# Two 16-head attentions of a float32 model: outputs ahead of the next copy on VectorE, and their transposes tile by tile

## The chip, the core and the metric

The kernel runs as one launch on one core of a Trainium2 chip. The metric is the device time of that launch in microseconds (us), as the median over runs. PE is TensorE, DVE is VectorE, ACT is ScalarE, POOL is GpSimd, SP is the queue that issues the DMAs.

## What is computed

A residual stream of 256 tokens by 1024 channels goes through four layers in float32: two with attention and a gated feed-forward network, and two with a mixer and a mixture of 32 experts. The part that the change touches is the attention of the first two layers (16 attention maps each), cut to what matters:

```python
# layer 0: 8 dilated heads and 8 forgetting heads of 64 channels
p = softmax(q @ k.T + mask)                   # mask differs by head
o[:, a*64:(a+1)*64] = p @ v[:, a]             # 16 heads -> 1024 channels
h = h + o @ w_out
# layer 1: 8 differential heads, each of two maps, v of 128 channels
o = (softmax(q1 @ k1.T + mask) - lam * softmax(q2 @ k2.T + mask)) @ v
o = rms_norm(o, subln_g) * (1 - lam_init)     # per head, over its 128 channels
h = h + o.reshape(256, 1024) @ w_out
```

The mixers of layers 2 and 3 hold, among other things, an attention of 8 latent heads each.

## The kernel before

Each engine has a program written out by hand, and semaphores join them; an engine takes its instructions in that order. Weights come as chunks of 1 MB through a ring of three buffers. For a product to be exact enough, each operand is split into a high and a low part (ACT writes the high one, DVE subtracts for the low one), and PE does three products for one (`product`).

**The attention** (`attention` in the programs of DVE and PE, `softmaxes` in that of ACT). For a map a, PE multiplies the scores (`pair_scores`, two maps at a time), DVE adds the mask and takes the row maximum (`scores`, L873), ACT takes the exponential and the row sum (L533), PE transposes the probabilities in three pieces (`turn`, L1495), DVE copies them out of PSUM (`probs`, L883) after a reciprocal of the row sums (L880), and PE multiplies them by v (`values`, L1505 to L1507). After every second map DVE scales the pair's two outputs out of PSUM into `tok` (`outputs`: L901 for heads of 64 channels; L906 and L908, with lambda, for the differential heads). The loop of DVE over the maps is

```python
for a in range(n):
    if a + 2 < n:
        scores(a + 2)
    if a + 1 < n:
        probs(a + 1)
    outputs(a)          # does something for odd a only
```

and that of PE, for each a: the scores of a later pair (at even a), `turn(a + 1)`, `values(a)`. In the differential attention ACT squares a finished pair's outputs after the exponential of an odd map (`head_squares`, L546: the pair before the one whose exponential it has just done), and POOL turns the sums into a factor and multiplies it in (L437, L438, L442); for the last pair DVE does the last part (`last_head_norm`, L935). The differential attention also multiplies its reciprocals of odd maps by lambda on DVE (L888).

**After the attention** the 256 x 1024 outputs in `tok` have to be transposed for the projection: 8 tiles of 128 channels, 2 transposes each (`transposes`, L1421). PE waits there until all of `tok` is ready. A tile k goes to the bank and half that `t_place(k)` gives; four tiles share two banks' worth of events. ACT reads each tile from PSUM as its high part (`high`, L508), DVE as its low part (`low`, L834); PE's projection (`out_projection`, `group`, L1358 to L1360) waits for the low part of tile k before its product k. The first half of the output channels uses banks 0 and 1 and two chunks of weights, the second half banks 2 and 3 and two more. ACT and DVE split those later chunks (`plain` and DVE's `out_projection`) after their tiles.

All four attentions, those of the latent heads too, use the same `attention` functions; only the two with 16 maps use `pair_scores`.

Of the kernel before, what the change touches and what calls it, by code (L numbers as in the profile page):

```python
# [18 lines left out]
F32 = mybir.dt.float32  # L19
F32R = mybir.dt.float32r  # L20
ALU = mybir.AluOpType
ACT = mybir.ActivationFunctionType
# [123 lines left out]
T_BASE = [sum(T_TILES[:q]) for q in range(len(T_TILES) + 1)]  # L146
T_BANKS = [2 * (n // 3) for n in T_TILES]
T_BANK_BASE = [sum(T_BANKS[:q]) for q in range(len(T_BANKS) + 1)]
# [3 lines left out]
def t_place(k):  # L152
    return 2 * (k // 4) + k % 2, k % 4 // 2

T_L0, T_L0O, T_F0, T_L1, T_L1O, T_F1 = range(6)
# [6 lines left out]
def build(nc, x, stream, router, small, const, fgain, out):  # L162
    es = ExitStack()
    with es:
# [302 lines left out]
        def _(act):  # L467
# [31 lines left out]

            def high(q, dst, gain, free):  # L500

                act.wait_ge(chunk_used, free) if free else None
                for k in range(T_TILES[q]):
                    b, at = t_place(k)
                    act.wait_ge(t_done, T_BANK_BASE[q] + b + 1)
                    if at:
                        act.wait_ge(t_low, T_BASE[q] + k - 1)
                    nc.scalar.activation(dst[:, k, :], B[4 + b][:, at * S:at * S + S], ACT.Copy, scale=gain(k)).then_inc(t_high, 1)  # L508

# [195 lines left out]
            projections(C_DIFF, 4, 16)  # L705
            softmaxes(16, range(2, 16), head_squares)
            head_squares(17)
            high(T_L1O, xh, lambda k: gain_sub[:, 0:1], C_DIFF_OUT)
            plain(C_DIFF_OUT, 3)
# [87 lines left out]
        def _(dve):  # L797
# [31 lines left out]

            def low(q, dst, hi, gain):  # L830
                for k in range(T_TILES[q]):
                    b, at = t_place(k)
                    dve.wait_ge(t_high, T_BASE[q] + k + 1)
                    stt(dst[:, k, :], B[4 + b][:, at * S:at * S + S], gain(k), hi[:, k, :].bitcast(F32),  # L834
                        ALU.mult, ALU.subtract).then_inc(t_low, 1)
# [29 lines left out]
            def attention(first, n, masks, scale, dv, diff, between=None, score_bank=0, turned_bank=6, score_banks=2):  # L865
# [11 lines left out]
                def probs(a):  # L877
                    dve.wait_ge(p_tr, first + a + 1)
                    step[0] += 1
                    nc.vector.reciprocal(rden[:, a, :], den[:, a, :]).then_inc(dve_step, 1)  # L880
                    if a >= 2:
                        dve.wait_ge(pv_done, first + a - 1)
                    nc.vector.tensor_copy(prT[:, a % 2, :], B[turned_bank + a % 2][:, 0:384]).then_inc(pT_ready, 1)  # L883

                    if diff and a % 2:
                        dve.wait_ge(dve_step, step[0])
                        step[0] += 1
                        ts(rden[:, a, :], rden[:, a, :], lamb[:, 6:7], None, ALU.mult).then_inc(dve_step, 1)  # L888
                    scale_step[a] = step[0]

                def outputs(a):
# [15 lines left out]
                    dve.wait_ge(dve_step, step[0])  # L907
                    tt(tok[:, :, a // 2 * dv:(a // 2 + 1) * dv], both[:, 0], both[:, 1], ALU.add).then_inc(o_done, 2)  # L908

# [6 lines left out]
                def rest():  # L916
                    probs(0)
                    for a in range(n):
                        if a + 2 < n:
                            scores(a + 2)  # L920
                        if a + 1 < n:
                            probs(a + 1)
                        outputs(a)
                        if between is not None:
                            between(a)
                    dve.wait_ge(o_done, first + n)
# [3 lines left out]
            def last_head_norm():  # L930

                dve.wait_ge(hrs_ready, 8)
                for t in range(NT):
                    o = tok[:, t, 7 * P:8 * P]
                    ins = ts(o, o, hrs[:, 14 + t:15 + t], None, ALU.mult)  # L935
                dve.wait_ge(head_normed, 7)
                ins.then_inc(tok_ready, 2)
# [304 lines left out]
            projections(C_DIFF, 4, kinds1, start)  # L1242
            rest()
            last_head_norm()
            low(T_L1O, xl, xh, lambda k: gain_sub[:, 0:1])
            out_projection(C_DIFF_OUT)
# [106 lines left out]
        def _(pe):  # L1353
# [40 lines left out]
            def run(steps):  # L1394
                for _ in steps:
                    pass
# [17 lines left out]
            def transposes(q, src, need, nk=KT, sem=None):  # L1414

                pe.wait_ge(tok_ready if sem is None else sem, need)
                for b in range(T_BANKS[q]):
# [4 lines left out]
                    ins.then_inc(t_done, 1)  # L1422

            def ready(q):
                pe.wait_ge(t_low, T_BASE[q + 1])
# [107 lines left out]

            def out_projection(c0, q):
                for half in range(2):
                    run(group(c0 + 2 * half, 2, [B[2 * half][:, :], B[2 * half + 1][:, :]], 512, None if half else q,
                              bank_done))

# [249 lines left out]
            pe.wait_ge(const_in, 16)  # L1788
            transposes(T_L0O, tok, tokens_ready())
            out_projection(C_HYB_OUT, T_L0O)  # L1790
            normed_transposes(T_F0)
# [7 lines left out]
            rest()  # L1799
            transposes(T_L1O, tok, tokens_ready())  # L1800
            out_projection(C_DIFF_OUT, T_L1O)
            normed_transposes(T_F1)
# [312 lines left out]
```

## Time and profile before

| | us |
|---|---|
| median of 3 runs | 1394.65 (1394.26 to 1394.74) |
| the profiled execution's own time | 1396.2 |
| its span, first to last instruction | 1394.2 |
| layer 0: attention | about 92 to 118 |
| layer 0: projection of its outputs | about 120 to 142 |
| layer 1: attention | about 415 to 449 |
| layer 1: projection of its outputs | about 454 to 477 |
| PE busy over the span | 1286.8 (92%) |
| DVE busy | 662.3 (48%) |
| ACT busy | 548.2 (39%) |
| mean granted clock of PE | 0.976 |

A view of the profile that lists instructions in time gives the start, the busy time, the engine, the line and the tiles (written <- read) with the shape; in square brackets stands how long the engine was idle before it and what ended that wait. A run of equal instructions is one row with its count. The chain of waits gives for each step its start and how long it was the step that everything waited for. The granted clock of PE is 1.00 at its full 2.4 GHz and 0.50 at 1.2 GHz.

### The profile page before, as it was taken

The page shows a single profiled execution, that of the slowest core. Times are in us where ns is not written, and L with a number is a line of the kernel's source. Part 1 is how long each engine was busy: PE and PEld are TensorE (multiplying, and loading weights), DVE is VectorE, ACT ScalarE, POOL GpSimd, SP SyncE. Part 2 cuts the span into 40 slices and gives each one's busy share as a digit, 9 for nine tenths or more (in the row PEclk, how much of TensorE's full clock was granted, in tenths as well). Part 3 has the DMA queues.
Part 4 walks back from the last instruction along what each step waited for, and adds up shares of the span by engine and source line. Part 5 has one row for each costly group of instructions (what it writes and reads, how often), then busy time and mean ns, then how long its engine had stood idle before and what let it go on. Part 6 is the DMA issues. An engine that isn't in the chain of part 4 may idle for free.

```text
span 1394.2 us, 19006 instructions
## 1 busy us (share of the span) xinstructions
PE 1286.8 (92%) x7252; PEld 932.3 (67%) x7252; DVE 662.3 (48%) x1321; ACT 548.2 (39%) x1072; POOL 36.7 (3%) x75
## 2 busy tenths in 40 slices
PE   7999899999996899999899789999879987999986
PEld 5878899997875799999777544344357874443432
DVE  6656666666757566666666621111056463110102
ACT  5455544445445554444656311111044641111101
POOL 0000000000003000000200000000000000000000
PEclk9999999999999999999999999999999898999999
DMA  9532455554550265555432969999974096999995
GB/s 344 182 121 91 139 190 184 181 181 151 181 181 1 92 210 182 186 187 185 139 122 105 378 256 423 420 420 421 422 264 153 23 387 228 416 422 421 421 421 232
DMA packets 68570, 336.80 MB, mean 242 GB/s; under 512 B 7888, under 2 KB 8016, under 8 KB 47376
## 3 DMA queue, kind: packets, MB, share of 16 engines
q1 hardware_dynamic: 68400, 335.50, 64.2%
q8 instruction: 48, 0.79, 0.2%
q0 software_dynamic: 96, 0.30, 0.1%
q14 instruction: 26, 0.21, 0.0%
HBM read 334.72 MB, written 1.05 MB: 241 GB/s over the span
## 4 chain that ended last, share of the span: by engine, by line
PE 76%; DVE 7%; DMA 7%; ACT 5%; issue 2%; POOL 1%; SPq 1%; DVEq 0%; ACTq 0%; POOLq 0%
PE bank L1358 15%; PE bank L1360 15%; PE bank L1359 15%; PE bank L1649 13%; DMA expert_part<-stream 7%; PE bank L1676 6%; PE bank L1606 2%; DVE w_low L815 2%; PE bank L1495 1%; ACT tok L497 1%; PE bank L1689 1%; ACT w_high L487 1%; ACT probs L533 1%; PE bank L1434 1%; PE bank L1410 1%
## 5 line engine op out<-in xcount | busy, mean ns | idle before, releaser
L815 DVE TENSOR_TENSOR w_low<-raw,w_high 128x1024 fp32r<-128x1024 f32 (+1 forms) x246 | 285.5, 1211 | 131.3 <-ACT w_high L487 131.0
L487 ACT ACTIVATE w_high<-raw 128x1024 fp32r<-128x1024 f32 (+1 forms) x246 | 241.6, 1042 | 43.6 <-PE bank L1360 43.2
L1649 PE MATMUL bank<-expert_part,slots_x 128*64 128x512 f32 x1024 | 233.0, 593 | 9.3 <-DMA expert_part<-stream 8.1
L1358 PE MATMUL bank<-x_high,w_high 128*128 128x256 f32 (+1 forms) x712 | 203.2, 285 | 3.8 <-DVE x_low L834 3.5
L1359 PE MATMUL bank<-x_low,w_high 128*128 128x256 f32 (+1 forms) x712 | 202.7, 285 | 0.0
L1360 PE MATMUL bank<-x_high,w_low 128*128 128x256 f32 (+1 forms) x712 | 202.7, 285 | 0.0
L1649 PEld LDWEIGHTS bank<-expert_part,slots_x 128*64 128x64 f32 x1024 | 76.8, 137 | 159.0 <-issue 138.2
L1358 PE MATMUL bank<-w_high,x_high 128*128 128x512 f32 (+1 forms) x416 | 163.3, 393 | 5.1 <-DVE x_low L834 3.2
L1359 PE MATMUL bank<-w_low,x_high 128*128 128x512 f32 (+1 forms) x416 | 161.2, 387 | 0.0
L1360 PE MATMUL bank<-w_high,x_low 128*128 128x512 f32 (+1 forms) x416 | 160.9, 387 | 0.0
L1125 DVE SCALAR_TENSOR_TENSOR expert_hid<-expert_gate,combine,bank 128x256 f32<-128x256 f32 x32 | 15.4, 481 | 304.8 <-ACT expert_gate L640 304.8
L1358 PEld LDWEIGHTS bank<-x_high,w_high 128*128 128x128 f32 (+1 forms) x712 | 137.0, 192 | 7.2 <-issue 4.2
L1359 PEld LDWEIGHTS bank<-x_low,w_high 128*128 128x128 f32 (+1 forms) x712 | 136.9, 192 | 0.8
L1360 PEld LDWEIGHTS bank<-x_high,w_low 128*128 128x128 f32 (+1 forms) x712 | 137.0, 192 | 0.2
L1676 PE MATMUL bank<-expert_part,hid_turned 128*64 128x512 f32 x512 | 116.9, 598 | 3.8 <-ACT hid_turned L644 3.8
L640 ACT ACTIVATE expert_gate<-bank 128x256 f32<-128x256 f32 x32 | 12.3, 384 | 273.6 <-PE bank L1649 273.6
L1358 PEld LDWEIGHTS bank<-w_high,x_high 128*128 128x128 f32 x416 | 78.5, 189 | 23.5 <-DVE w_low L815 4.8
L1360 PEld LDWEIGHTS bank<-w_high,x_low 128*128 128x128 f32 x416 | 78.4, 188 | 15.3
L1359 PEld LDWEIGHTS bank<-w_low,x_high 128*128 128x128 f32 x416 | 78.4, 189 | 14.3
L1676 PEld LDWEIGHTS bank<-expert_part,hid_turned 128*64 128x64 f32 x512 | 33.9, 136 | 63.7 <-issue 54.8
L1360 PE MATMUL bank<-w_high,hid_low 128*128 128x512 f32 x176 | 69.5, 395 | 0.0
L1359 PE MATMUL bank<-w_low,hid_high 128*128 128x512 f32 x176 | 69.4, 394 | 0.0
(249 smaller groups left out, 1572.2 us busy)
## 6 DMA issues: line engine op xcount, KB each, us to landing
expert_part<-stream SPq DMA_DIRECT2D x164, 1024.0 KB, 17.9
raw<-stream SPq DMA_DIRECT2D x244, 512.0 KB, 5.2
expert_part<-stream SPq DMA_DIRECT2D x56, 512.0 KB, 17.8
const_sb<-const SPq DMA_DIRECT2D x1, 2070.0 KB, 13.4
residual<-x SPq DMA_DIRECT2D x2, 512.0 KB, 4.1
final_gain<-fgain SPq DMA_DIRECT2D x2, 512.0 KB, 8.8
out<-residual SPq DMA_DIRECT2D x2, 512.0 KB, 2.9
small_sb<-small SPq DMA_DIRECT2D x1, 765.0 KB, 5.9
```

Source lines behind the costliest of these rows:

```text
L487: nc.scalar.activation(wh[:, u, cols], raw[:, u, cols], ACT.Copy).then_inc(w_high, 1)
L497: nc.scalar.activation(tok[:, t, cols], h[:, t, cols], ACT.Square, scale=float(D) ** -0.5, accum_out=ssq[:, t, half:half + 1]).then_inc(ss ...
L533: ins = nc.scalar.activation(pr[:, a % 2, lo:hi], sm[:, a % 2, lo:hi], ACT.Exp, bias=nmax[:, a, t:t + 1], scale=-1.0, accum_out=den[:, a, ...
L815: tt(wl[:, u, cols], raw[:, u, cols], wh[:, u, cols].bitcast(F32), ALU.subtract).then_inc(w_low, 1)
L1125: stt(m_hidden[:, :], m_gate[:, :], comb[:, p:p + 1], B[0][:, DE:2 * DE], ALU.mult, ALU.mult).then_inc(m_hid, 1)
L1358: mm(o, ah, bh, start=start, stop=False, **kw)
L1359: mm(o, ah, bl, start=False, stop=False, **kw)
L1360: return mm(o, al, bh, start=False, stop=stop, **kw)
L1410: ins = nc.tensor.transpose(B[4 + b][:, at:at + P], tok[:, t, k * P:(k + 1) * P], ident)
L1606: ins = mm(o[:, kk * 4 * CAP:(kk + 1) * 4 * CAP], src[:, t, k * P:(k + 1) * P], pick[:, g % 2, t, :], start=kk == 0 and t == 0 and src is ...
L1649: ins = mm(B[0][half * CAP:(half + 1) * CAP, :], xg[p // 4 % 2][:, k, x_of], w[k % 4 // 2][:, k % 2 * 512:(k % 2 + 1) * 512], start=k == 0 ...
L1676: ins = mm(B[2 + col][rows, :], hidT[:, k, rows], slot[slot_of(i)][k][:, col * 512:(col + 1) * 512], start=p % 2 == 0 and k == 0, stop=p % ...
```

## The change

Four things are done, the first two in the attention and the last two behind it.

1. DVE's loop calls `outputs(a)` before `probs(a + 1)`.
2. The reciprocal is taken once for a pair, at its odd map; the multiplication of the reciprocals by lambda is gone, and the last addition of the differential heads becomes a multiply-and-add with lambda as its per-partition scalar. These and point 1 also hold for the two attentions of latent heads (which have no lambda).
3. Seven of the eight tiles of the attention's outputs are transposed by a new function that waits for the heads of a group of tiles, in banks 4, 6, 7 and 2 in place of 4 to 7, without a wait for the last pair. The eighth tile (the last pair) is transposed in the midst of the projection, after its first chunk of weights.
4. In the differential layer ACT reads the first two tiles before it squares the last pair, and DVE takes the low parts of five tiles before the last head's norm.

```diff
+T_BY_TILE = (1, 4)
+T_BANKS = [5 if q in T_BY_TILE else 2 * (n // 3) for q, n in enumerate(T_TILES)]
+def t_bank(q, b):
+    return (4, 6, 7, 2)[b] if q in T_BY_TILE else 4 + b
+def t_event(q, k):
+    return T_BANK_BASE[q] + (5 if q in T_BY_TILE and k == 7 else t_place(k)[0] + 1)
...
             softmaxes(16, range(2, 16), head_squares)
+            high(T_L1O, xh, lambda k: gain_sub[:, 0:1], C_DIFF_OUT, range(2))
             head_squares(17)
-            high(T_L1O, xh, lambda k: gain_sub[:, 0:1], C_DIFF_OUT)
+            high(T_L1O, xh, lambda k: gain_sub[:, 0:1], 0, range(2, 8))
...
                 def probs(a):
                     dve.wait_ge(p_tr, first + a + 1)
-                    step[0] += 1
-                    nc.vector.reciprocal(rden[:, a, :], den[:, a, :]).then_inc(dve_step, 1)
+                    if a % 2:
+                        step[0] += 1
+                        nc.vector.reciprocal(rden[:, a - 1:a + 1, :], den[:, a - 1:a + 1, :]).then_inc(dve_step, 1)
+                        scale_step[a] = step[0]
                     if a >= 2:
                         dve.wait_ge(pv_done, first + a - 1)
                     nc.vector.tensor_copy(prT[:, a % 2, :], B[turned_bank + a % 2][:, 0:384]).then_inc(pT_ready, 1)
-
-                    if diff and a % 2:
-                        dve.wait_ge(dve_step, step[0])
-                        step[0] += 1
-                        ts(rden[:, a, :], rden[:, a, :], lamb[:, 6:7], None, ALU.mult).then_inc(dve_step, 1)
-                    scale_step[a] = step[0]
...
-                    tt(tok[:, :, a // 2 * dv:(a // 2 + 1) * dv], both[:, 0], both[:, 1], ALU.add).then_inc(o_done, 2)
+                    stt(tok[:, :, a // 2 * dv:(a // 2 + 1) * dv], both[:, 1], lamb[:, 6:7], both[:, 0], ALU.mult, ALU.add)\
+                        .then_inc(o_done, 2)
...
+                        outputs(a)
                         if a + 1 < n:
                             probs(a + 1)
-                        outputs(a)
...
             rest()
+            low(T_L1O, xl, xh, lambda k: gain_sub[:, 0:1], range(5))
             last_head_norm()
-            low(T_L1O, xl, xh, lambda k: gain_sub[:, 0:1])
+            low(T_L1O, xl, xh, lambda k: gain_sub[:, 0:1], range(5, 8))
...
+            def tile_transposes(q, done, counts):
+                for b in range(4):
+                    if b % 2 == 0:
+                        pe.wait_ge(done, counts[b // 2])
+                    for k in (k for k in range(7) if t_place(k)[0] == b):
+                        for t in range(NT):
+                            at = t_place(k)[1] * S + t * P
+                            ins = nc.tensor.transpose(B[t_bank(q, b)][:, at:at + P], tok[:, t, k * P:(k + 1) * P], ident)
+                    ins.then_inc(t_done, 1)
+            def last_tile(q, done, count):
+                pe.wait_ge(done, count)
+                pe.wait_ge(t_low, T_BASE[q] + 6)
+                for t in range(NT):
+                    ins = nc.tensor.transpose(B[t_bank(q, 3)][:, S + t * P:S + (t + 1) * P], tok[:, t, 7 * P:8 * P], ident)
+                ins.then_inc(t_done, 1)
...
+                    for j in group(c0 + 2 * half, 2, [B[2 * half][:, :], B[2 * half + 1][:, :]], 512, None if half else q,
+                                   bank_done):
+                        if last is not None and half == 0 and j == 0:
+                            last_tile(q, last, count)
...
-            transposes(T_L0O, tok, tokens_ready())
-            out_projection(C_HYB_OUT, T_L0O)
+            tokens_ready()
+            tile_transposes(T_L0O, o_done, (8, 14))
+            out_projection(C_HYB_OUT, T_L0O, o_done, 16)
...
-            transposes(T_L1O, tok, tokens_ready())
-            out_projection(C_DIFF_OUT, T_L1O)
+            tokens_ready()
+            tile_transposes(T_L1O, head_normed, (4, 7))
+            out_projection(C_DIFF_OUT, T_L1O, tok_ready, toks[0])
```

The order of DVE's instructions in layer 0's attention, two maps long, before the change (ISA is the masked score and its row maximum, COPY the probabilities, and TENSOR_TENSOR the pair's outputs):

```order
L880 RECIPROCAL rden<-den 128x2 [waits probs_transposed]
L883 COPY probs<-bank 128x384 [waits pv_done]
L901 TENSOR_TENSOR tok<-bank,rden 128x2x128 [waits pv_done,dve_step]
L873 ISA scores_masked,neg_max<-bank,const_sb 128x128 [waits probs_ready,scores_done]
L873 ISA neg_max 128x1
L873 ISA scores_masked,neg_max<-bank,const_sb 128x256
L873 ISA neg_max 128x1
L880 RECIPROCAL rden<-den 128x2 [waits probs_transposed]
L883 COPY probs<-bank 128x384 [waits pv_done]
```

and the same stretch with the change, with its own line numbers:

```order
L907 TENSOR_TENSOR tok<-bank,rden 128x2x128 [waits pv_done,dve_step]
L895 COPY probs<-bank 128x384 [waits pv_done,probs_transposed]
L883 ISA scores_masked,neg_max<-bank,const_sb 128x128 [waits probs_ready,scores_done]
L883 ISA neg_max 128x1
L883 ISA scores_masked,neg_max<-bank,const_sb 128x256
L883 ISA neg_max 128x1
L891 RECIPROCAL rden<-den 128x4 [waits probs_transposed]
L895 COPY probs<-bank 128x384 [waits pv_done]
```

The copy of the pair's next map has moved behind the outputs, between them and the next scores; one reciprocal of two is gone.

On PE, behind layer 1's attention, before (L1505 to L1507 are the last map's values, L1421 the transposes of `tok`, L1358 to L1360 the projection):

```order
L1505 MATMUL bank<-v,probs 128x128 [waits probsT_ready]
L1506 MATMUL bank<-v,probs 128x128
L1507 MATMUL bank<-v,probs 128x128
L1421 MATMUL bank<-const_sb,tok 128x128 [waits tok_ready]
L1421 MATMUL bank<-const_sb,tok 128x128 x15
L1358 MATMUL bank<-w_high,x_high 128x512 [waits t_low_ready,w_low_ready]
```

and with the change, from the last values to the first product of the projection, and from the end of its first chunk to the second:

```order
L1532 MATMUL bank<-v,probs 128x128 [waits probsT_ready]
L1533 MATMUL bank<-v,probs 128x128
L1534 MATMUL bank<-v,probs 128x128
L1440 MATMUL bank<-const_sb,tok 128x128 [waits heads_normed]
L1440 MATMUL bank<-const_sb,tok 128x128 x7
L1440 MATMUL bank<-const_sb,tok 128x128 [waits heads_normed]
L1440 MATMUL bank<-const_sb,tok 128x128 x5
L1366 MATMUL bank<-w_high,x_high 128x512 [waits t_low_ready,w_low_ready]
...
L1448 MATMUL bank<-const_sb,tok 128x128 [waits t_low_ready,tok_ready]
L1448 MATMUL bank<-const_sb,tok 128x128
L1366 MATMUL bank<-w_high,x_high 128x512 [waits t_low_ready,w_low_ready]
```

Fourteen of the sixteen transposes wait for heads that ended earlier, and two stand behind the first chunk's 24 products.

## Rows read from the trace of the kernel before

**Rows 1.** Busy time and granted clock (PEclk) of four stretches.

```profile
core 0: us, PE busy (x) PEld busy (x) DVE busy (x) ACT busy (x) POOL busy (x), PEclk, DMA share, GB/s
92.40:116.00 23.60, 22.70 (x191) 18.95 (x191) 19.66 (x94) 13.81 (x56) 0.00 (x0) 1.00 0.09 32
415.00:447.00 32.00, 24.18 (x199) 19.57 (x196) 25.80 (x110) 17.47 (x84) 9.28 (x20) 1.00 0.06 22
447.30:451.10 3.80, 0.05 (x1) 0.00 (x0) 1.60 (x4) 0.69 (x4) 1.81 (x4) 0.69 0.00 0
1104.10:1114.30 10.20, 10.20 (x48) 9.63 (x46) 3.99 (x16) 2.99 (x10) 0.00 (x0) 0.50 0.14 34
```

**Rows 2.** Instructions in time, layer 0's attention, values of map 11 to values of map 13.

```profile
111.64 0.33 PE L1505 MATMUL bank<-v,probs 128*128 128x64 f32 x2
...
112.56 0.42 DVE L901 TENSOR_TENSOR tok<-bank,rden 128x256 f32<-128x256 f32 x1
...
112.90 0.28 DVE L873 CUSTOM_DVE_ANT_0 scores_masked<-bank,stick_qkT 128x128 f32<-128x128 f32 x1
...
113.28 0.40 ACT L533 ACTIVATE probs<-scores_masked,neg_max 128x128 f32<-128x128 f32 x1 [0.67 <-PE bank L1495]
...
113.53 0.54 DVE L883 COPY probs<-bank 128x384 f32<-128x384 f32 x1
...
113.98 0.28 DVE L873 CUSTOM_DVE_ANT_0 scores_masked<-bank,stick_qkT 128x128 f32<-128x128 f32 x1
...
114.32 0.55 PE L1495 MATMUL bank<-const_sb,probs 128*128 128x128 f32 x3 [0.49 <-ACT probs L533]
...
114.70 0.33 PE L1505 MATMUL bank<-v,probs 128*128 128x64 f32 x2
```

**Rows 3.** The chain of waits, layer 1's attention, one pair (start, length, what).

```profile
427.79 0.70 DVE rope_a L906
...
428.58 0.44 DVE tok L908
...
...
429.74 0.88 ACT probs L533 x4
...
430.67 0.55 PE bank L1495 x3
...
432.00 0.70 DVE rope_a L906
```

**Rows 4.** Groups by line: busy us, mean ns of one, idle us before.

```profile
L834 DVE SCALAR_TENSOR_TENSOR x_low<-bank,gain_sub,x_high 128x256 fp32r<-128x256 f32 x8 | 3.5, 479 | 2.5 <-ACT x_high L508 2.5
L908 DVE TENSOR_TENSOR tok<-rope_a 128x256 f32<-128x256 f32 x8 | 3.4, 426 | 0.8
```

**Rows 5.** Instructions in time, the end of layer 0's attention.

```profile
116.67 0.43 PE L1505 MATMUL bank<-v,probs 128*128 128x64 f32 x2
...
118.38 1.94 PE L1421 MATMUL bank<-const_sb,tok 128*128 128x128 f32 x16 [0.83 <-DVEq L1227]
119.11 0.85 ACT L508 ACTIVATE x_high<-bank,const_sb 128x256 fp32r<-128x256 f32 x2 [3.75 <-PE bank L1421]
119.61 0.88 DVE L834 SCALAR_TENSOR_TENSOR x_low<-bank,const_sb,x_high 128x256 fp32r<-128x256 f32 x2 [1.50 <-ACT x_high L508]
...
121.01 0.40 PE L1358 MATMUL bank<-w_high,x_high 128*128 128x512 f32 x1
```

**Rows 6.** Instructions in time, layer 1's last pairs and its projection's start.

```profile
443.67 0.39 PE L1505 MATMUL bank<-v,probs 128*128 128x128 f32 x2
...
444.61 0.69 DVE L906 TENSOR_TENSOR rope_a<-bank,rden 128x512 f32<-128x512 f32 x1
...
445.82 0.54 DVE L883 COPY probs<-bank 128x384 f32<-128x384 f32 x1
...
446.41 0.49 PE L1505 MATMUL bank<-v,probs 128*128 128x128 f32 x2 [0.92 <-DVE probs L883]
...
451.11 3.67 PE L1421 MATMUL bank<-const_sb,tok 128*128 128x128 f32 x16 [3.76 <-DVE tok L935]
...
455.75 0.40 PE L1358 MATMUL bank<-w_high,x_high 128*128 128x512 f32 x1
```

More of the change, by code:

```diff
@@ L146 @@
 T_BASE = [sum(T_TILES[:q]) for q in range(len(T_TILES) + 1)]
-T_BANKS = [2 * (n // 3) for n in T_TILES]
+T_BY_TILE = (1, 4)
+T_BANKS = [5 if q in T_BY_TILE else 2 * (n // 3) for q, n in enumerate(T_TILES)]
 T_BANK_BASE = [sum(T_BANKS[:q]) for q in range(len(T_BANKS) + 1)]
@@ L498, in rms, with high @@
                                          accum_out=ssq[:, t, half:half + 1]).then_inc(ssq_ready, 1)
-            def high(q, dst, gain, free):
+            def high(q, dst, gain, free, tiles=None):
                 act.wait_ge(chunk_used, free) if free else None
-                for k in range(T_TILES[q]):
+                for k in range(T_TILES[q]) if tiles is None else tiles:
                     b, at = t_place(k)
-                    act.wait_ge(t_done, T_BANK_BASE[q] + b + 1)
+                    act.wait_ge(t_done, t_event(q, k))
                     if at:
                         act.wait_ge(t_low, T_BASE[q] + k - 1)
-                    nc.scalar.activation(dst[:, k, :], B[4 + b][:, at * S:at * S + S], ACT.Copy, scale=gain(k)).then_inc(t_high, 1)
+                    nc.scalar.activation(dst[:, k, :], B[t_bank(q, b)][:, at * S:at * S + S], ACT.Copy, scale=gain(k)).then_inc(t_high, 1)
             def one(k):
@@ L828, in normed, with low @@
                     ts(tok[:, 1, cols], h[:, 1, cols], rstd[:, 1:2], None, ALU.mult).then_inc(tok_ready, 1)
-            def low(q, dst, hi, gain):
-                for k in range(T_TILES[q]):
+            def low(q, dst, hi, gain, tiles=None):
+                for k in range(T_TILES[q]) if tiles is None else tiles:
                     b, at = t_place(k)
                     dve.wait_ge(t_high, T_BASE[q] + k + 1)
-                    stt(dst[:, k, :], B[4 + b][:, at * S:at * S + S], gain(k), hi[:, k, :].bitcast(F32),
+                    stt(dst[:, k, :], B[t_bank(q, b)][:, at * S:at * S + S], gain(k), hi[:, k, :].bitcast(F32),
                         ALU.mult, ALU.subtract).then_inc(t_low, 1)
@@ L1532, in attention, with out_projection @@
                 return start, rest
-            def out_projection(c0, q):
+            def out_projection(c0, q, last=None, count=None):
                 for half in range(2):
-                    run(group(c0 + 2 * half, 2, [B[2 * half][:, :], B[2 * half + 1][:, :]], 512, None if half else q,
-                              bank_done))
+                    for j in group(c0 + 2 * half, 2, [B[2 * half][:, :], B[2 * half + 1][:, :]], 512, None if half else q,
+                                   bank_done):
+                        if last is not None and half == 0 and j == 0:
+                            last_tile(q, last, count)
             def down(c, off, buf, last, first=False):
```

## Prediction

> **What bounds the kernel now.** First the stretches: layer 0's attention loop has PE busy 22.70 of 23.60 us at full clock and DVE 19.66, so PE sets the pace there; layer 1's has PE busy 24.18 of 32.00 and DVE 25.80, so no engine is full and a ring of waits must set it [rows 1]. Next the instructions in time. A pair of layer 0 takes 3.06 us, from the values of map 11 at 111.64 to those of map 13 at 114.70 [rows 2]. In layer 1 the chain of waits shows the ring: the outputs' multiplication at 427.79, the addition at 428.58, ACT's squares until 429.74, then its exponential, PE's turn at 430.67, and the next multiplication at 432.00, so 4.21 us a pair [rows 3]. Last, the ends of both attentions. In layer 0 the values of map 15 begin at 116.67, the 16 transposes at 118.38, and the projection's fourth multiplication at 121.01 [rows 5]. In layer 1 the values begin at 446.41, PE waits 3.76 us for the last head's norm, the clock granted there is a mean of 0.69, the 16 transposes take 3.67 us where layer 0's take 1.94, and the fourth multiplication starts at 455.75 [rows 1, 5, 6]. The change shortens both ends and, as I read it, lengthens both loops.
>
> **The change part by part.** The sum is made against the profiled execution, 1396.2 us (span 1394.2 and 2.0 around it). The median of the runs, 1394.65, is 1.55 lower; I carry the difference over to it.
>
> *Outputs ahead of the copy, layer 0.* After the change the copy for map a+1, and behind it the next scores, wait until PE has done the values of map a. That closes a ring: values to outputs 0.92 (111.64 to 112.56); outputs to the next DVE operation 0.34 (112.56 to 112.90); copy to the next scores 0.45 (113.53 to 113.98); scores to exponential 0.38 (112.90 to 113.28); exponential to PE's turn 1.04 (113.28 to 114.32); turn to values 0.38 (114.32 to 114.70) [rows 2]. This is 3.51 against 3.06, so +0.45 a pair, over 6 periods from map 1 to map 13: +2.7. PE's 4% of idle time in the loop cannot hide it, since the ring has nothing left over. The last pair, map 13 to map 15, took 1.97 (114.70 to 116.67 [rows 2, 5]). Now it is 0.92, then 0.34, then copy to values 0.59 (445.82 to 446.41 [rows 6]), then one more copy of 0.54 with a reciprocal, some 0.73: 2.58, so +0.6. The first pair has one reciprocal less on its way, −0.1. Layer 0's loop: **+3.2**.
>
> *The same in layer 1.* Values to multiplication 0.94 (443.67 to 444.61 [rows 6]), multiplication to addition 0.79 [rows 3], the addition as a multiply-and-add with a scalar 0.39 to the next operation, then 0.45, 0.38, 1.04 and 0.38 as above: 4.37 against 4.21, +0.16 a pair, six times: +1.0. The 0.39 is layer 0's 0.34 and 0.05 more: the nearest row for the new form is L834's multiply-and-add of the same 256 columns, 479 ns, where today's addition takes 426 [rows 4]. Its ends are 0 and +0.05; I take +0.05. The squares' old ring becomes 4.21 + 0.05 = 4.26 and stays just under. The last pair took 2.74 (443.67 to 446.41 [rows 6]); now 0.94 + 0.79 + 0.39 + 0.59 + 0.73 = 3.44, +0.7. Layer 1's loop: **+1.6**.
>
> *Reciprocals and lambda.* They go from DVE, which has free time in both loops (19.66 of 23.60, 25.80 of 32.00 [rows 1]). I cost them at nothing; if DVE were the bound they would be worth under 0.3 us a pair.
>
> *Layer 0's end.* Let s be the start of the last values. Before: transposes at s + 1.71, a product's fourth multiplication at s + 4.34, thus, with 0.23 a multiplication at full clock, a start worth s + 3.65. Now the transposes of the earlier heads follow the values, at s + 0.73 (six multiplications), high of tile 0 is 0.73 behind the first transpose (118.38 to 119.11), low 0.50 later (119.11 to 119.61), the product about 0.54 after that [rows 5]: s + 2.5. The late tile stands in the projection: two transposes at 0.12, +0.24. **−0.9**.
>
> *Layer 1's end.* Before: 455.75 − 3 × 0.23 = 455.06, so s + 8.65 [rows 6]. Now 14 transposes, at 0.12 while the clock stays up, run from s + 0.7 to s + 2.4. DVE has the last outputs' multiplication at s + 0.95, and the multiply-and-add until s + 2.2, so low of tile 0 begins at s + 2.3 and the first product at s + 2.84. The others come at about 0.45 a tile against 0.69 a product (three multiplications), in time. With the late tile 0.24, and 0.1 for a DVE that now has five tiles before the norm: 8.65 − 2.84 − 0.34 = **−5.5**. What hides the norm: squares, POOL and DVE's last part took until about 4.6 us after s, and the late tile is wanted only behind the first chunk's seven products, 8 × 0.69 = 5.5 after the first product, at s + 8.4. If that cover went, PE would stand there for the rest. ACT's and DVE's splitting of the next chunk comes later than now, relative to PE, by the same shift; I find 1.3 us of margin, and cost it at nothing.
>
> *Latent attentions.* Two more, with the copy behind the outputs too. The bounds are 0 (hidden) and layer 0's +0.45 at each of their few pairs' slack; I take +0.3 for each attention: **+0.6**. DMAs and their issuing queues are not moved in any part.
>
> Sum: 3.2 + 1.6 − 0.9 − 5.5 + 0.6 = −1.0. So 1395.2 on the execution's own scale and 1393.7 on the median's. A measurement of this kernel can tell 0.2%, 2.8 us, from no change: the bounds are 1391.9 and 1397.4.
>
> **A rule that speaks against it.** In layer 0, the 16 transposes ran at 0.12 us each behind a short stand of PE, and the multiplications after them at 0.23; in layer 1, they ran at 0.23 each behind 3.76 us of standing, and the clock was half [rows 5, 6]. I read that as the long stand having brought the clock down. The Trainium skill, "TensorE: Matmul & The Clock Gate", section "Part 4: PE-mode transpose", says that a transpose does not count as PE-busy for the clock in the same way. By it 14 transposes right behind thin values might let the clock fall even without a stand, and −5.5 would be some −2.7; the trace of layer 0 does not bear it out, as its transposes kept the clock. That is rival D.
>
> **The rivals.**
>
> A, *half-clock stretches elsewhere move.* PE runs at 0.50 from 1104.1 to 1114.3 though it is busy all the time [rows 1]. Such a stretch starts from a stand of PE before it, and any shift of work against the clock's own beat can end it, or start one. If it goes wholly, 10.2 us become 5.1. The place is far from the change, so against it speaks only that nothing there moves by itself; for it, that everything behind layer 0 shifts by microseconds. It gives 2 to 5 us: about 1390, 1388.6 to 1391.8, faster. 0.28.
>
> B, *the clock falls inside the loops.* PE stands longer in every pair, about 0.45 more in layer 0. If the granted clock falls to half there for the attention, turn to values goes from 0.38 to 0.64 and values to outputs from 0.92 to 1.5 (the multiplications' part doubled), some +0.8 a pair, seven pairs: +5.8, so 1399.5, slower. It decides as soon as one loop's granted clock is near 0.5 instead of 1.00. Against it: layer 1's loop already has PE idle for a quarter of the time, and is granted 1.00 [rows 1]. 0.10.
>
> C, *the delay is hidden.* If the copy of map a+1 was late anyway, both loops keep their periods: 3.06 and 4.21. Then the +4.8 is not paid: 1389, faster. Against it stands the ring above, whose every part is a row. 0.08.
>
> D, *the clock falls at layer 1's end all the same*, by the transposes or by the few products: transposes 0.23, first products at half. It gives back some 2.8: 1396.5, still within 0.2%. 0.04. That the change does not do what it says I leave out as a rival: the order of instructions shows it done.
>
> **How the numbers follow.** Forecast 0.50 at 1393.7, of which nearly all is within 0.2%; its own range is 1391.5 to 1396, by the ends of the terms (the loop's +0.45 times 6 could be +0.2 or +0.6 a pair; latent ones 0 to +1.5). A 0.28 and C 0.08 are faster, D 0.04 is the same, B 0.10 slower. That makes faster 0.36, same 0.54, slower 0.10. The range takes in A, C's upper part and D: 1388.5 to 1397.0; it leaves out B and the tail of A.
>
> **What would show it.** Layer 0's values of maps 11 and 13 should be 3.5 us apart, layer 1's 4.4, with PE waiting for ACT's probabilities in every pair and DVE's copy directly behind the outputs. Behind layer 1's last values the transposes should follow at once, at 0.12 each and a granted clock of 1.00, the first product about 2.8 us after the values' start, the late tile's two between the first chunk and the second with no wait. Periods of 3.06 and 4.21 would mean C; a clock near 0.5 in a loop, B; transposes at 0.23 there, D; and 1104 to 1114 at full clock, A. A wait of PE at the late tile or the third chunk would mean that my margin was wrong.

## Result: slower by 0.45%, and the profile after

The changed kernel takes 1400.56 us (median of 20 runs, 1397.58 to 1409.75), the kernel before 1395.03 in the same session (20 runs, 1394.04 to 1398.15). The ratio, worked out over all these runs, is 1.0045 with a 95% interval of 1.0032 to 1.0058, so 6.3 us slower (the two medians alone are 5.5 us apart). The forecast was 1393.7, no change, with a range of 1388.5 to 1397.0; the time is outside it.

The profiled execution took 1401.66 us, its span is 1399.7. Busy time of PE is 1295.0 us (1286.8 before), DVE 657.9, ACT 548.9; PE's mean granted clock is 0.972 (0.976 before).

Busy time and granted clock of five stretches of the kernel after; columns as in [rows 1]:

```profile
92.40:116.00 23.60, 20.85 (x172) 16.91 (x173) 16.07 (x76) 11.85 (x49) 0.00 (x0) 1.00 0.09 33
116.20:126.40 10.20, 9.70 (x45) 9.02 (x44) 4.38 (x17) 3.64 (x13) 0.00 (x0) 0.50 0.00 0
415.00:447.00 32.00, 26.14 (x187) 19.53 (x185) 21.38 (x79) 18.59 (x74) 7.51 (x15) 1.00 0.11 37
454.20:457.00 2.80, 2.28 (x19) 2.02 (x18) 2.08 (x5) 1.98 (x8) 0.87 (x3) 1.00 0.00 0
1106.00:1126.50 20.50, 19.32 (x84) 17.97 (x84) 10.25 (x27) 8.30 (x18) 0.00 (x0) 0.50 0.49 178
```

Layer 0's loop still runs at 1.00, but PE is busy 20.85 of 23.60 us where it was 22.70 [rows 1]. Then, at 116.2, the clock is at 0.50 for 10.2 us, where the trace before has 1.00. The stretch of half clock at 1104, 10.2 us before [rows 1], is 20.5 us long. At layer 1's end it is the other way round: 0.69 before, 1.00 now.

Instructions in time, one pair of layer 0's attention after (maps 9 to 11), beside [rows 2]:

```profile
110.00 0.55 PE L1522 MATMUL bank<-const_sb,probs 128*128 128x128 f32 x3 [0.41 <-ACT probs L542]
110.38 0.33 PE L1532 MATMUL bank<-v,probs 128*128 128x64 f32 x2
...
111.30 0.42 DVE L907 TENSOR_TENSOR tok<-bank,rden 128x256 f32<-128x256 f32 x1 [1.00 <-PE bank L1534]
111.64 0.55 DVE L895 COPY probs<-bank 128x384 f32<-128x384 f32 x1
...
112.10 0.28 DVE L883 CUSTOM_DVE_ANT_0 scores_masked<-bank,rope_a 128x128 f32<-128x128 f32 x1
...
112.49 0.40 ACT L542 ACTIVATE probs<-scores_masked,neg_max 128x128 f32<-128x128 f32 x1 [1.46 <-DVE neg_max L883]
...
113.53 0.55 PE L1522 MATMUL bank<-const_sb,probs 128*128 128x128 f32 x3 [0.41 <-ACT probs L542]
113.91 0.33 PE L1532 MATMUL bank<-v,probs 128*128 128x64 f32 x2
```

From values to values it is 3.53 us (110.38 to 113.91), and PE waits 0.41 for ACT: the ring that the forecast worked out as 3.51. The next pair, maps 11 to 13, takes 3.84 (113.91 to 117.75 below), as the clock falls in it.

The chain of waits in layer 1's attention after, beside [rows 3], and the groups beside [rows 4]:

```profile
433.41 0.70 DVE rope_a L912
434.16 0.04 issue
434.20 0.49 DVE tok L914
434.72 0.69 ACT rope_a L555 x4
435.41 0.05 issue
435.45 0.99 ACT probs L542 x4
436.45 0.04 issue
436.49 0.55 PE bank L1522 x3
...
437.81 0.70 DVE rope_a L912
```

The groups of the two multiply-and-adds:

```profile
L914 DVE SCALAR_TENSOR_TENSOR tok<-rope_a,lam 128x256 f32<-128x256 f32 x8 | 3.9, 484 | 0.8
L844 DVE SCALAR_TENSOR_TENSOR x_low<-bank,gain_sub,x_high 128x256 fp32r<-128x256 f32 x8 | 3.5, 479 | 3.8 <-ACT x_high L517 3.8
```

The pair takes 4.40 us, 4.21 before. The chain still goes by the squares, with the addition at 0.48 in place of 0.43 and ACT's exponential 0.1 longer on the path. The forecast had this ring at 4.26 and the new one, by the copy and the scores, at 4.37; in the trace the squares end at 435.42 and the scores' maximum at 435.36, so both rings end within 0.1 us of each other, and which of them sets the pair is not shown. Lambda's addition takes 484 ns; its nearest row had 479.

Instructions in time, the ends of both attentions after, beside [rows 5, 6]:

```profile
115.77 0.43 PE L1532 MATMUL bank<-v,probs 128*128 128x64 f32 x2 [0.61 <-DVE probs L895]
...
117.75 0.53 PE L1532 MATMUL bank<-v,probs 128*128 128x64 f32 x2
...
120.21 0.69 PE L1532 MATMUL bank<-v,probs 128*128 128x64 f32 x2 [0.44 <-DVE probs L895]
...
121.54 0.63 PE L1532 MATMUL bank<-v,probs 128*128 128x64 f32 x2
...
122.82 3.19 PE L1440 MATMUL bank<-const_sb,tok 128*128 128x128 f32 x14
...
125.67 0.78 PE L1366 MATMUL bank<-w_high,x_high 128*128 128x512 f32 x1
...
453.62 0.39 PE L1532 MATMUL bank<-v,probs 128*128 128x128 f32 x2
...
454.29 1.69 PE L1440 MATMUL bank<-const_sb,tok 128*128 128x128 f32 x14
...
456.51 0.47 PE L1366 MATMUL bank<-w_high,x_high 128*128 128x512 f32 x1 [0.52 <-DVE x_low L844]
...
462.08 0.38 PE L1448 MATMUL bank<-const_sb,tok 128*128 128x128 f32 x2
```

Layer 1's end went as worked out: first product 2.89 us behind the last values' start (forecast 2.84), the 14 transposes at 0.12 each, the late tile with no wait. Layer 0's end lies in the half-clock stretch, which begins with the values of map 12: 14 transposes in 3.19 us, and the first product at 125.67, where the kernel before has it at 120.24. That is 5.4 later; the forecast's terms for this place (3.2 - 0.9, less the late tile, which comes after) make some 2.1.

### The profile page after: what moved, and what is told of

It reads as the page before. It is cut to its first block, busy times and chain, and to the rows that moved or that the text cites. A ratio compares the mean times of both kernels' runs of the same rounds, so it can differ in the third digit from the quotient of the medians.

```text
span 1399.7 us, 18996 instructions
## 1 busy us (share of the span) xinstructions
PE 1295.0 (93%) x7252; PEld 937.8 (67%) x7252; DVE 657.9 (47%) x1289; ACT 548.9 (39%) x1072; POOL 36.7 (3%) x75
## 4 chain that ended last, share of the span: by engine, by line
PE 76%; DVE 7%; DMA 7%; ACT 6%; issue 2%; POOL 1%; SPq 0%; DVEq 0%; ACTq 0%; POOLq 0%
PE bank L1366 15%; PE bank L1368 14%; PE bank L1367 14%; PE bank L1678 13%; DMA expert_part<-stream 7%; PE bank L1705 6%; PE bank L1635 2%; DVE w_low L825 2%; ACT probs L542 1%; PE bank L1522 1%; PE bank L1418 1%; PE bank L1718 1%; ACT w_high L496 1%; ACT tok L506 1%; PE bank L1461 1%
## 5 line engine op out<-in xcount | busy, mean ns | idle before, releaser
L649 ACT ACTIVATE expert_gate<-bank 128x256 f32<-128x256 f32 x32 | 12.3, 384 | 273.9 <-PE bank L1678 273.9
```

## Experiments

Three theories were tried. Theory 1: the outputs' place costs more than its rings, since it makes PE stand in every pair and PE is then granted half clock for longer, at layer 0's end and (theory 1b) around the latent attention of layer 3. Theory 2: the extra half clock is chance. Theory 3: the new transposes bring it down. All ratios are to the kernel before, timed on the same chip; 0.001 is 1.4 us.

| | median us | ratio (95%) | half clock at about 116 | near 1100 |
|---|---|---|---|---|
| after | 1400.56 | 1.0045 (1.0032 to 1.0058) | 10.2 us | 20.5 us |
| e1_old_order | 1389.40 | 0.9957 (0.9944 to 0.9969) | none | 17.1 |
| e2_loops_only | 1407.67 | 1.0093 (1.0079 to 1.0107) | 10.2 | 20.5 |
| e3_again | 1401.73 | 1.0045 (1.0026 to 1.0064) | 6.8 | 20.5 |
| e4_filled | 1402.43 | 1.0053 (1.0040 to 1.0066) | none | 20.5 |
| e5_old_l0 | 1397.54 | 1.0013 (1.0000 to 1.0026) | none | 20.5 |
| e6_old_l1 | 1399.48 | 1.0020 (1.0003 to 1.0037) | 10.2 | 20.5 |
| e7_old_latent | 1396.15 | 1.0013 (0.9999 to 1.0026) | none | 17.1 |
| e8_before_again | 1395.82 | 1.0001 (0.9992 to 1.0010) | 3.4 | 10.2 |
| e9_filled_products | 1402.12 | 1.0048 (1.0035 to 1.0061) | none | 20.5 |
| e10_tails_only | 1389.28 | 0.9950 (0.9937 to 0.9963) | none | 10.2 |
| e11_tile_early | 1394.43 | 0.9987 (0.9973 to 1.0001) | none | 17.1 |
| e12_filled_again | 1400.54 | 1.0032 (1.0020 to 1.0044) | none | 20.5 |
| e13_latent_alone | 1393.16 | 0.9976 (0.9967 to 0.9985) | none | 20.5 |
| e14_l0_alone | 1394.17 | 0.9989 (0.9979 to 0.9999) | none | 20.5 |
| e15_l0_filled | 1393.12 | 0.9981 (0.9967 to 0.9995) | none | 10.2 |

The last two columns are from the one profiled execution of each, read as the length in us of the stretch whose granted clock is 0.50. The kernel before has none at 116 and 10.2 near 1100. e3 is the changed kernel once more, e8 the kernel before, e12 the same as e4. Differences between two rows of the table have an interval of some 2 to 2.6 us either way.

**The old order in the changed kernel** (PE's wait for the first transposes is for the outputs of map 13, since bank 4 holds them):

```diff
-                        outputs(a)
                         if a + 1 < n:
                             probs(a + 1)
+                        outputs(a)
```

> The changed kernel with DVE's copy ahead of the outputs again in all attentions; the pair's reciprocal, lambda in the sum and the tiles' transposes stay. Theory 1 (the outputs' place lengthens both loops, makes PE stand in every pair of layer 0, and by that brings its clock to half for 10 us from 116 on): the pair takes 3.06 us in layer 0 and 4.2 in layer 1, no half clock before 140, and the time is 1395.0 - 0.9 - 5.5 = 1388.6, between 1387 and 1390. Theory 2 (where half-clock stretches fall is chance from one execution to the next, and the order's own price is only the forecast 5.4): 1395 or so less 5.4 from the measured 1400.6, with half-clock stretches anywhere. Theory 3 (the new transposes themselves bring the clock down in layer 0): the half clock at 116 stays, and the time is 1392.

Measured: 0.9957, 12.3 us under the changed kernel (0.0088). Theory 3 falls: the new transposes are in, and the clock is 1.00 from 116 to 126, by the stretch of that name:

```profile
116.00:126.00 10.00, 9.76 (x56) 8.24 (x56) 4.38 (x11) 3.81 (x9) 0.00 (x0) 1.00 0.01 2
```

The moved outputs alone cost 12.3 us, with an interval of about 2.5 either way, not the 5.4 forecast that theory 2 would leave them.

**Loops only**: `probs`, `outputs` and the loop of the changed kernel in the kernel before, whose `transposes` stay.

```diff
+                        outputs(a)
                         if a + 1 < n:
                             probs(a + 1)
-                        outputs(a)
```

> The kernel before with the first two parts of the change alone: outputs ahead of the copy, one reciprocal a pair, lambda in the sum; the old transposes of all 16 tiles. Theory 1: 3.5 us a pair in layer 0 and 4.4 in layer 1, half clock again from about 116, and 1395.0 + 5.4 + 3.5 = 1404, between 1402 and 1406. Theory 2: no half clock at 116 in this execution, 1400.4. Theory 3: never half clock at 116, 1400.4.

Measured: 1407.67, 13.0 us over the kernel before (0.0093) and slower than even theory 1 had it. The half clock at 116 is there without any new transpose (the stretch):

```profile
116.40:126.60 10.20, 8.66 (x40) 7.91 (x40) 3.52 (x13) 2.82 (x11) 0.00 (x0) 0.50 0.00 0
```

Against the changed kernel it gives the new transposes' worth: 0.0048, 6.7 us.

**The changed kernel again.**

> The changed kernel once more. Theory 1: the clock falls to half within 0.5 us of 116 again, and layer 0's first product starts 5.4 us after that of the kernel before; median 1400.5; only the stretches far behind differ in length (one of 20.5 us at 1106 may be 10.2 again, some 3 to 5 us less). Theory 2: the half clock at 116 is absent or elsewhere, and the first product is 2.3 us after that of the kernel before.

Measured: 1401.73. The clock falls again, but at 117.7 and for 6.8 us, and the first product is 4.7 later than before, not 5.4. So the fall recurs while its place and length vary.

**PE's idle time filled**, with transposes (twice) and with products:

```diff
                         values(a)
+                        if by_pair and not diff and a < 14 and (a % 2 == 0 or a > 10):
+                            for j in range(3 if a % 2 == 0 else 6):
+                                nc.tensor.transpose(B[turned_bank + a % 2][:, j % 3 * P:(j % 3 + 1) * P], ident, ident)
```

In e9 the added line is a product:

```diff
-                                nc.tensor.transpose(B[turned_bank + a % 2][:, j % 3 * P:(j % 3 + 1) * P], ident, ident)
+                                mm(B[turned_bank + a % 2][:, j % 3 * P:j % 3 * P + 64], ident, ident[:, 0:64], start=True, stop=True)
```

> The changed kernel with PE's idle time in layer 0's attention filled: three transposes of the identity into a PSUM bank already read, after the values of each even map, and six after those of maps 11 and 13; they change no result. Theory 1: PE no longer stands, the granted clock is 1.00 to beyond 126, layer 0's first product starts about 2.3 us after that of the kernel before in place of 5.4, and the time is 1400.5 - 3.5 = 1397. Theory 2: as the changed kernel, 1400.5 within 1. If the added transposes do not count as work for the clock, the fall at 116 stays as well.

> The filled kernel with products in place of the added transposes: matmuls of the identity by 64 of its columns, at the same places and in the same number. If transposes count less for the clock than products, this one keeps layer 0's clock in more of its executions than the kernel filled with transposes: a median under 1399. If what fills the gap does not matter, or the loss is only moved behind layer 0, it is 1402 as well.

> The kernel filled with transposes once more, since its one profiled execution was the shortest of its five: if it keeps the clock in layer 0 in every execution, no half clock at 116 again, and the loss lies behind; if its other executions fell at 116, it may show here. Median 1402 within 1.5 either way.

Measured: the clock holds at 116 in all three, and with transposes the first product comes 2.4 us after that of before, as expected (with products 4.0 after). The stretch in e4:

```profile
116.20:126.40 10.20, 9.90 (x69) 8.56 (x69) 6.20 (x20) 4.82 (x15) 0.00 (x0) 1.00 0.01 2
```

and filled with products:

```profile
116.20:126.40 10.20, 9.96 (x79) 9.24 (x79) 6.41 (x22) 4.75 (x15) 0.00 (x0) 1.00 0.01 2
```

But the medians, 1400.5 to 1402.4, are those of the changed kernel; the expected 3 us did not show in the time. In e4's trace the half-clock stretch at 794 is 13.7 us and that at 1029 is 10.2, where the changed kernel's first trace has 10.2 and 6.8; but e9 and e12 have 10.2 and 6.8 there too, and the changed kernel again (e3) 13.7 and 10.2. So the local gain is there in the profiled executions, and what the whole run gains of it stayed open.

**One attention put back at a time**, here the latent ones; in e5 the condition is `first`, in e6 `first != 16`, with PE's wait as in e1:

```diff
-                        outputs(a)
+                        if first < 32:
+                            outputs(a)
                         if a + 1 < n:
                             probs(a + 1)
+                        if not (first < 32):
+                            outputs(a)
```

> The changed kernel with the copy ahead of the outputs again in layer 0's attention alone. The sum of places: layer 0's loop is 3.2 shorter and its clock stays (3 to 3.5 more), so its projection starts 1 us before that of the kernel before, and the time is 1400.6 - 6.5 = 1394. The other possibility, seen with the filled kernel: what layer 0 gains is given back behind it in longer half-clock stretches (at 797, 1030 and 1105), and the time stays above 1397.

> The changed kernel with the copy ahead of the outputs again in layer 1's attention alone. 4.2 us a pair there in place of 4.4, no change of the clock in it: 1.6 less than the changed kernel, 1399. If the clock plays a part there too, more than 3 less.

> The changed kernel with the copy ahead of the outputs again in the two latent attentions alone. Theory 1b: the new order there is what lengthens the half-clock stretch at 1105 from 10 to 20 us, as it brings the clock down in layer 0: the stretch is 10 again, the place behind it comes 3 us earlier, and the time is 1400.6 - 0.6 - 3 = 1397. Rival: that stretch's length is chance or hangs on the position alone: still 17 to 20 us, and 1400.

Measured against the changed kernel: layer 0 is worth 4.5 us (0.0032), layer 1 3.5 (0.0025), the latent attentions 4.5 (0.0032), each with an interval of about 2.5 us either way; together 12.4, as e1 has it. Layer 0's 4.5 is under the 6.5 of the sum of places. The surprise is the latent attentions, forecast at 0.6. In e7 the clock did not fall at 116 although layer 0 has the new order, so that fall is frequent, not certain, and part of what these differences of medians hold may be how often it came. The stretch near 1100 shrank to 17.1 us, not to 10.

**The kernel before again.**

> The kernel before once more, for the half-clock stretches far behind the change. If theory 1b holds: 10 us at 1104 again; if length is chance: 10 to 20 us. Time 1395.5 either way, 1393 to 1398.

Measured: 1395.82, and 10.2 us at 1105 again. It also shows 3.4 us of half clock at 118.6, so a short fall there is not the new order's alone.

**The transposes alone**: the kernel before with points 3 and 4 of the change, a reciprocal a map, and one wait more:

```diff
-            transposes(T_L0O, tok, tokens_ready())
+            tokens_ready()
+            tile_transposes(T_L0O, o_done, (14, 14))
...
+            pe.wait_ge(o_done, 30)
+            tile_transposes(T_L1O, head_normed, (4, 7))
```

> The kernel before with the transposes tile by tile and the late tile alone: a reciprocal a map, lambda on the reciprocals, copy ahead of the outputs. If the pair's reciprocal is worth nothing: 1389.4 within 1. If it is what made the half-clock stretch at 1105 17 us where the kernel before has 10: that stretch is 10 again and the time is 1388.

Measured: 1389.28, ratio 0.9950, 7.0 us faster than before; with e1 it is the fastest kernel of the study. The pair's reciprocal and lambda in the sum (e1 against e10, 0.9957 to 0.9950) make no difference that can be told. The stretch is 10.2 us again.

**The eighth tile early**, on e1, in bank 3 and without the wait for the low parts:

```diff
+                    if last is not None and half == 0:
+                        last_tile(q, last, count)
                     run(group(c0 + 2 * half, 2, [B[2 * half][:, :], B[2 * half + 1][:, :]], 512, None if half else q,
                               bank_done))
```

> The changed kernel in the old order of DVE, and the eighth tile transposed ahead of the projection, behind the other seven, in bank 3. Layer 0: its last heads are there before the seven tiles are done, no loss. Layer 1: the last head's norm ends about 4.5 us behind the last values' start, so the first product starts 4.8 behind it in place of 2.8: 2 us more, and PE stands for 2 of them; without a fall of the clock 1391.5, with one 1393. If the gain came from the earlier tiles alone, no loss: 1389.4.

Measured: 1394.43, 4.2 us over e1 (0.0030, about 2.6 us either way). Instructions in time at its layer 1 end:

```profile
445.10 2.05 PE L1443 MATMUL bank<-const_sb,tok 128*128 128x128 f32 x14
449.48 0.44 PE L1450 MATMUL bank<-const_sb,tok 128*128 128x128 f32 x2 [2.34 <-DVE tok L945]
...
450.35 0.63 PE L1371 MATMUL bank<-w_high,x_low 128*128 128x512 f32 x1
```

PE waits 2.34 us for the last head's norm, and right behind it the products take 0.63 us in place of 0.39, at half clock for 3.4 us. The late place of the eighth tile saves the 2.34 us of waiting, and the stand seems to bring the clock down on top; this trace alone shows it.

**One part alone, on e10**: the outputs first where `first >= 32` (e13) or `first == 0` (e14), and e14 with the filling of e4 (e15).

```diff
+                        if first >= 32:
+                            outputs(a)
                         if a + 1 < n:
                             probs(a + 1)
-                        outputs(a)
+                        if not (first >= 32):
+                            outputs(a)
```

> The kernel with only the transposes changed (1389.3), and in the two latent attentions alone the outputs ahead of the copy. Theory 1b: the half-clock stretch at 1096 is 20.5 us in place of 10.2, the projection behind it starts about 3.5 us later, and the time is 1389.3 + 0.6 + 3.5 = 1393.4. Rival (its length depends on what layers 0 and 1 did): 10 us, 1390.

> The kernel with only the transposes changed, and in layer 0's attention alone the outputs ahead of the copy. The loop costs 3.2; with a fall of the clock at 116 in most executions 3 more: 1395.5, between 1394 and 1397. If the fall costs nothing in the end, as the filled kernels' medians would have it: 1392.5. The stretch at 1099 stays at 10.2 us in either case.

> The one with the new order in layer 0 alone, with PE's idle time there filled by transposes of the identity. If the fall at 116 is what costs: no half clock there, and 1392.5, 3 less than without the filling. If the filling only moves the loss: the same as without it, within 1.

Measured: the latent attentions alone cost 3.6 us (0.0026, 2.2 either way), as theory 1b had it. The half-clock stretch near 1100 in e10:

```profile
1095.20:1105.40 10.20, 10.20 (x47) 9.63 (x47) 3.69 (x16) 2.64 (x9) 0.00 (x0) 0.50 0.09 14
```

and in e13:

```profile
1097.00:1117.50 20.50, 19.26 (x85) 17.90 (x85) 10.24 (x28) 8.30 (x18) 0.00 (x0) 0.50 0.46 179
```

and PE's instructions in time in e13 there:

```profile
1108.13 0.85 PE L1528 MATMUL bank<-const_sb,probs 128*128 128x128 f32 x3
1109.48 0.69 PE L1538 MATMUL bank<-v,probs 128*128 128x64 f32 x2 [0.50 <-DVE probs L893]
...
1113.04 3.67 PE L1435 MATMUL bank<-const_sb,tok 128*128 128x128 f32 x16 [0.74 <-DVEq L1353]
```

In e10 half clock begins among the small products of the other mixers, and full clock is back as the attention ends, so its 16 transposes take 1.97 us; in e13 the same 16 take 3.67. PE's wait of 0.50 us for the copy that now queues behind the outputs ends only at 1109.48, 12.5 us into the stretch. The first 10.2 us of it, as long as e10's whole stretch, have no wait of PE:

```profile
1097.00:1107.20 10.20, 10.20 (x47) 9.63 (x47) 2.84 (x13) 1.23 (x5) 0.00 (x0) 0.50 0.00 0
```

So that wait is not what kept the clock down at 1107.2. e14, with the old order in the latent attentions, has 20.5 us there too, where 10.2 was expected, and 15.5 us of it before PE waits at all:

```profile
1098.80:1114.30 15.50, 15.50 (x71) 14.75 (x70) 5.81 (x20) 5.44 (x12) 0.00 (x0) 0.50 0.23 87
```

From the first of those mixers' 128 x 64 products to the projection's first product it is 17.63 us in e10, 20.19 in e14 and 20.55 in e13. So the long stretch costs 2.6 us at this place with the old order, and the new order adds 0.4, near the 0.3 that the forecast had for it. What e13 shows of theory 1b is thus the long stretch and the price, not that the new order made it. e13's trace also has 6.8 us of half clock at 144.6, long before the latent attentions, that e10's lacks.

Layer 0 alone costs 5.4 us (0.0039, 2.3 either way), between the two expected. Its trace has no fall at 116: the first product is at 123.08 against e10's 119.45, 3.6 us of plain waiting. The filled version, 1393.12 against 1394.17, is 1 us less, inside the intervals; and since e14's trace had no fall at 116 either, it can't say what the filling does to one.

## Why the prediction was wrong

*The rings.* Right in size. Layer 0's pair takes 3.53 us (forecast 3.51), layer 1's 4.40 (4.37), and PE waits for ACT in both. In layer 1 the squares' ring, forecast at 4.26, came out as long as the new one, so the number there has some luck in it. The parts of layer 1's loop, 1.0 and 0.7, make 1.7 and not the 1.6 in the sum. e14's first product of layer 0's projection is 3.6 us behind e10's, where the forecast's loop has 3.2.

*Reciprocals and lambda at nothing.* Right: e1 and e10 differ by less than can be told.

*Both ends.* Right: -0.9 and -5.5 forecast, 6.4 together; e10 measured 7.0, e2 against the changed kernel 6.7. In e10 layer 0's first product is 0.8 earlier than before's. The cover of the last norm held: the late tile found everything ready, and e11 shows what it costs without it.

*Latent attentions, +0.6.* This term was mis-sized most: 3.6 alone, 4.5 put back. As a ring it was about right (0.4 for the attention of layer 3 at equal clock, by e13 and e14); what the step left out is the clock.

*The clock.* The step that failed is the forecast's case as a whole: outside the two ends it took the granted clock as given, a term of 0 in the sum. The order's rings came to 5.4 forecast, yet the order costs 12.3. The 6.9 us between go with half-clock time, in two readings. In the traces, half clock adds up to 65.5 us in e1 and 78.7 in the changed kernel; at most half of the 13.2 more is lost, an estimate of up to 6.6 us. In the runs, each with its mean granted clock, the changed kernel's 20 go from 1397.6 us at 0.977 to 1409.8 at 0.965, 1.0 us for 0.001 (0.9 by a line through all 20); on one chip the median clock is 0.977 for e1 and 0.972 for the changed kernel (e3), which makes 4.5 to 5 us. So -1.0 forecast, +6.3 measured: 6.9 from the order, the rest within the intervals. That the order costs this much and that the clock goes with it is shown; how it lowers the clock is not.

*The rivals.* B was of the right kind. That its time (1399.5) came near is partly luck: it had the clock fall for the whole of layer 0's loop. It fell only at the loop's last maps, from 116.2 on, after a wait of 0.61 us for a copy; a second wait of 0.44 came inside the stretch. Before that PE stood 0.41 us a pair at 1.00. Against B I had held layer 1, whose PE is idle a quarter of the time at 1.00; that row was no shield for layer 0. A had the stretch at 1104 as the place that can move, and counted its end only as a gain; it doubled. Nor does that stretch start from a stand of PE, as A had it. In the trace of before PE works at full clock without a wait for 11.9 us ahead of it:

```profile
1092.20:1104.10 11.90, 11.90 (x90) 10.38 (x90) 4.03 (x21) 6.47 (x22) 0.00 (x0) 1.00 0.01 1
```

The half-clock time of such a stretch can go both ways, and A had a price for one of them only. D did not come: layer 1's transposes ran at 0.12 at a granted 1.00. The Trainium skill's sentence that a transpose does not count as busy for the clock ("TensorE: Matmul & The Clock Gate", "Part 4: PE-mode transpose") is not borne out there. Nor is it by the fillings: the clock held at 116 in e4 and e12 with transposes, as it did in e9 with products. That is weaker evidence, as it held in two of six executions with nothing filled.

*Still open:* what brings the clock down at layer 0's end (it fell in 4 of 6 profiled executions with the new order and nothing filled, in none of 4 filled, and for 3.4 us in one of 7 with the old order), and why filling did not lower the medians. More profiled executions of one kernel would be needed.

## What to carry to other kernels

Before an instruction is moved ahead of another on an in-order engine, close the ring that it makes: here an output that nobody hurries for went ahead of a copy that PE waits for, and the ring that came of it was read from seven rows to 0.02 us. But such a change has to be priced in granted clock as well, over the whole kernel and not only where PE stands; here the price came out at twice that of the rings. So compare the mean granted clock of the runs before a difference of some microseconds is put down to instructions. When a change bundles several parts, take them apart: the transposes alone are 0.5% faster (e10), and the bundle 0.45% slower.

## What the runs showed that I had not expected

The length of one half-clock stretch near 1100 us took only the values 10.2, 17.1 and 20.5 us in 17 profiled executions. It was 20.5 in all nine with outputs first in the latent attention (seven kernels, two of them twice); with the copy first it was 10.2 in four (before, e8, e10, e15), 17.1 in three (e1, e7, e11) and 20.5 in one (e14).

That looks like the order's doing, but another thing sorts the lengths at least as well: how early the clock falls among the small products ahead of the attention. From the fall to the first transposes of probabilities behind those products it is 1.2 to 1.6 us in the four with 10.2, 1.8 to 1.9 in the three with 17.1, and 1.9 to 4.1 in the ten with 20.5 (4.1 in e14). Among the eight with the old order alone it holds without exception. Only e2 (1.87 and 20.5) and e7 (1.91 and 17.1) overlap; e2 waits for a copy inside the stretch and e7 does not, so there the wait may have made the last 3.4 us. No run moved the place of the fall by itself, so this is a reading and not shown.

The lengths also overstate the difference. All four executions with 10.2, and e2, have another 3.4 us of half clock further on (at 1145 in before, 41 us behind the start of the first), and no other has. From 10.2 to 20.5 it is thus 6.9 us more of half clock, and from 10.2 to 17.1 only 3.5, which fits that e1 and e10 can't be told apart by their medians.
